# Forget-gate logits of a two-layer trunk: from a TensorE weight chunk to VectorE multiply-and-sum operations

## What is computed

```
def odd_mixer(h, w_in, b_forget, w_out):
    proj = h @ w_in
    fq, fk, fv, fl = jnp.split(proj, [FOX_WIDTH, 2 * FOX_WIDTH, 3 * FOX_WIDTH], axis=-1)
    log_f = jax.nn.log_sigmoid(fl.astype(jnp.float32) + b_forget.astype(jnp.float32))
    o = forgetting_attention(split_heads(fq, FOX_HEADS), split_heads(fk, FOX_HEADS),
                             split_heads(fv, FOX_HEADS), log_f.transpose(0, 2, 1))
    return merge_heads(o).astype(h.dtype) @ w_out
```

## Time and profile before

| | us |
|---|---|
| timed runs, median of 3 (lowest, highest) | 1211.52 (1211.35, 1211.59) |
| profiled execution | 1210.91 |
| its span | 1209.1 |
| TensorE busy | 1197.1 |
| GpSimd busy | 516.9 |
| ScalarE busy | 392.4 |
| VectorE busy | 284.1 |

### The profile page before, as it was taken

The page is one execution under the profiler, slowest core; times in us unless marked ns, Lnnn a source line. Parts: engine busy times, 40 slices in busy tenths (PEclk is TensorE's granted clock), DMA queues, the critical chain, the costliest instruction groups (busy, mean ns, idle before and its releaser), DMA issues.

```text
span 1209.1 us, 14500 instructions
## 1 busy us (share of the span) xinstructions
PE 1197.1 (99%) x5578; PEld 989.9 (82%) x5578; DVE 284.1 (23%) x491; ACT 392.4 (32%) x616; POOL 516.9 (43%) x289
## 2 busy tenths in 40 slices
PE   8999999999999999999999999999999999999998
PEld 6888887898888888888888888678988888888886
DVE  3441056241111111000142325725211101110002
ACT  5122346453223332212242314634433223331210
POOL 5546521744444434444435443033643444435330
PEclk9999999999999999999999999999999999999999
DMA  7444203242223232322224422022322323222211
GB/s 268 132 124 146 95 7 100 70 145 100 100 91 104 87 104 88 103 94 98 70 88 141 173 96 79 18 70 87 105 102 90 104 87 104 88 103 94 98 53 70
DMA packets 34359, 120.14 MB, mean 99 GB/s; under 512 B 3683, under 2 KB 3939, under 8 KB 34316
## 3 DMA queue, kind: packets, MB, share of 16 engines
q1 hardware_dynamic: 30472, 110.46, 26.7%
q10 hardware_dynamic: 3844, 9.07, 2.8%
HBM read 116.09 MB, written 3.42 MB: 99 GB/s over the span
## 4 chain that ended last, share of the span: by engine, by line
PE 98%; DMA 1%; DVE 0%; ACT 0%; POOL 0%; SPq 0%; issue 0%; DVEq 0%; POOLq 0%
PE ps L979 30%; PE ps L981 30%; PE ps L980 30%; PE ps L1175 2%; PE ps L1141 2%; PE ps L1159 1%; PE ps L1006 1%; DMA w_raw<-weights 1%; PE ps L1276 0%; PE ps L1254 0%; PE ps L1139 0%; PE ps L1279 0%; PE ps L1266 0%; POOL w_lo L269 0%; PE ps L1338 0%; PE ps L1337 0%
## 5 line engine op out<-in xcount | busy, mean ns | idle before, releaser
L269 POOL TENSOR_TENSOR w_lo<-w_raw,w_hi 128x1024 fp32r<-128x1024 f32 x199 | 476.5, 2410 | 563.6 <-ACT w_hi L387 562.0
L979 PE MATMUL ps<-h_hi,w_hi 128*128 128x512 f32 (+1 forms) x1008 | 383.0, 380 | 0.0
L981 PE MATMUL ps<-h_hi,w_lo 128*128 128x512 f32 (+1 forms) x1008 | 382.0, 379 | 0.0
L980 PE MATMUL ps<-h_lo,w_hi 128*128 128x512 f32 (+1 forms) x1008 | 382.0, 379 | 0.0
L387 ACT ACTIVATE w_hi<-w_raw 128x1024 fp32r<-128x1024 f32 x201 | 210.1, 1056 | 325.3 <-DMA w_raw<-weights 318.2
L979 PEld LDWEIGHTS ps<-h_hi,w_hi 128*128 128x128 f32 x1008 | 189.6, 188 | 35.7 <-issue 0.3
L981 PEld LDWEIGHTS ps<-h_hi,w_lo 128*128 128x128 f32 x1008 | 189.6, 188 | 35.5
L980 PEld LDWEIGHTS ps<-h_lo,w_hi 128*128 128x128 f32 x1008 | 189.6, 188 | 35.4
L979 PE MATMUL ps<-w_hi,prod_hi 128*128 128x512 f32 x352 | 137.1, 390 | 0.0
L981 PE MATMUL ps<-w_hi,prod_lo 128*128 128x512 f32 x352 | 136.9, 389 | 0.0
L980 PE MATMUL ps<-w_lo,prod_hi 128*128 128x512 f32 x352 | 136.9, 389 | 0.0
(11 more groups left out here) (123 smaller groups left out, 715.2 us busy)
## 6 DMA issues: line engine op xcount, KB each, us to landing
w_raw<-weights SPq DMA_DIRECT2D x201, 512.0 KB, 3.2
x<-x_in SPq DMA_DIRECT2D x4, 512.0 KB, 6.6
gain_post<-norms ACTq DMA_DIRECT2D x4, 512.0 KB, 4.2
minus_f<-forget_rows ACTq DMA_DIRECT2D x1, 2048.0 KB, 11.5
gain_pre<-norms ACTq DMA_DIRECT2D x3, 512.0 KB, 4.1
out<-x SPq DMA_DIRECT2D x3, 512.0 KB, 2.6
bias_rows<-bias_row ACTq DMA_DIRECT2D x1, 1280.0 KB
rel<-bias_rows ACTq DMA_DIRECT2D x1, 1024.0 KB, 5.5
```

Source lines behind the costliest of these rows:

```text
L269: nc.gpsimd.tensor_tensor(w_lo[:, c % RING], w_raw[:, c % RING], w_hi[:, c % RING].bitcast(F32), ALU.subtract).then_inc(lo_done, 1)
L979: mm(to, held[0], moved[0], start=start, stop=False)
L980: mm(to, held[0], moved[1], start=False, stop=False)
L981: return mm(to, held[1], moved[0], start=False, stop=stop)
```

## The change

The gate chunk leaves the stream (200 chunks are left). The 8 gate columns come as rows (`gate_rows`, 8x1024), each broadcast to all 128 partitions: heads 0 to 3 into `gate_w_a`, heads 4 to 6 into `gate_w_b`, head 7 into `gate_w_last`, 4 MB in all, by ScalarE's queue. `boundary(2)` writes its normalized rows to `gate_x`, a buffer of four tiles, instead of `work`. VectorE forms the logits by `tensor_tensor_reduce` over 128x1024: for each group of four heads 16 operations (4 tiles by 4 heads), whose sums fill columns of `gate_z`. TensorE turns four 128x4 blocks of a group into a 4x512 row block (`turn_logits`), group 0 ahead of query/key chunk 1, group 1 ahead of chunk 10. The rest of the gate's work (bias, Exp, Ln, sum, store, spread, mask) is done once for each group on 4 rows or heads.

```diff
-            pe.wait_ge(lo_done, GATE1 + 1)
-
-            for k in range(KT):
-                mm(ps[:, 0, :], w_hi[:, GATE1 % RING, cols(k)], h_hi[:, k, :], start=k == 0, stop=False)
-                last = mm(ps[:, 0, :], w_hi[:, GATE1 % RING, cols(k)], h_lo[:, k, :], start=False, stop=k == KT - 1)
-            last.then_inc(chunk_used, 1)
+
+            def turn_logits(g):
+                pe.wait_ge(gate_dots, 16 * (g + 1))
+                pe.wait_ge(evacuated, qk_first)
+                for t in range(TILES):
+                    n = 16 * g + 4 * t
+                    last = nc.tensor.transpose(ps[0:4, 1 + 2 * g, cols(t)], gate_z[:, n:n + 4], ident[:])
+                last.then_inc(gate_turned, 1)
...
-                    if i == 3:
-                        pe.wait_ge(forget_logit, 1)
+                    if i in (1, 10):
+                        turn_logits(i // 10)
...
+            def dots(g, d0, d1):
+                for d in range(d0, d1):
+                    t, h = d // 4, d % 4
+                    n = 16 * g + d
+                    vec.wait_ge(gate_w_landed[g + (h == 3) if g else 0], 16)
+                    vec.wait_ge(normed, 4 * 2 + t + 1)
+                    if n:
+                        vec.wait_ge(gate_dots, n)
+                    else:
+                        vec.wait_ge(pre_summed, 4 * 2 + 4)
+                    held = gate_w_last[:] if g and h == 3 else gate_w[g][:, h, :]
+                    nc.vector.tensor_tensor_reduce(squares[:], gate_x[:, t, :], held, 1.0, 0.0, ALU.mult, ALU.add,
+                                                   gate_z[:, n:n + 1]).then_inc(gate_dots, 1)
...
+            dots(0, 0, 6)
+            copy_v(0)
+            dots(0, 6, 16)
+            copy_v(1)
+            copy_qk(0)
+            gate_logit(0)
+            dots(1, 0, 2)
+            copy_qk(1)
+            gate_scan(0)
+            dots(1, 2, 4)
+            for i in range(2, 8):
                 copy_qk(i)
...
+                dots(1, 2 * i, 2 * i + 2)
+            copy_qk(8)
+            copy_qk(9)
+            gate_logit(1)
+            add_masks(0)
+            copy_qk(10)
+            gate_scan(1)
+            for i in range(11, LATE):
+                copy_qk(i)
...
-                      {6: lambda: copy_qk(LATE), 9: lambda: copy_qk(LATE + 1)})
+                      {6: lambda: copy_qk(LATE), 9: lambda: copy_qk(LATE + 1), 11: lambda: add_masks(1),
+                       15: lambda: vec.wait_ge(f_masked, 8)})
...
+            act.wait_ge(chunk_used, AFTER[2] - 4)
+            act.dma_start(gate_w[0][:], gate_rows[0:4].partition_broadcast(P)).then_inc(gate_w_landed[0], 16)
+            act.dma_start(gate_w[1][:], gate_rows[4:7].partition_broadcast(P)).then_inc(gate_w_landed[1], 16)
             boundary(2)
...
+            act.dma_start(gate_w_last[:], gate_rows[7].partition_broadcast(P)).then_inc(gate_w_landed[2], 16)
...
+            highs(V1 + AHEAD, QK1 + 8)
+            gate_log(0)
+            high(QK1 + 8)
+            spread_rows(0)
+            highs(QK1 + 9, QK1 + 18)
+            gate_log(1)
+            high(QK1 + 18)
+            spread_rows(1)
+            highs(QK1 + 19, OUT1 + 5)
```

More of the change, by code:

```diff
@@ L73 @@
 V1 = FOUT0 + FT
-GATE1 = V1 + 8
-QK1 = GATE1 + 1
+QK1 = V1 + 8
 OUT1 = QK1 + 2 * FOX
@@ L186, in build @@
             sem(n) for n in ("forget_logit", "forget_log", "f_ready", "f_stored", "f_landed"))
+        gate_w_landed = [sem(f"gate_w_landed{n}") for n in range(3)]
+        gate_dots, gate_turned = sem("gate_dots"), sem("gate_turned")
         ret_k_turned, ret_k_scaled, ret_kv, ret_first, ret_second, ret_state = (
@@ L699, in pre @@
                 q = 4 * b + t
-                row = work[:, 2 * (t % 2):2 * (t % 2) + 2, :].rearrange("p a s -> p (a s)")
+                row = gate_x[:, t] if b == 2 else work[:, 2 * (t % 2):2 * (t % 2) + 2, :].rearrange("p a s -> p (a s)")
                 vec.wait_ge(gain_pre_landed, 16 * (b + 1))
@@ L704, in pre @@
                     vec.wait_ge(x_updated, q - 3)
-                if t >= 2:
+                if t >= 2 and b != 2:
                     vec.wait_ge(h_turned, q - 1)
@@ L915, in _, with gate_logit, gate_scan, copy_v @@
             boundary(2)
-            for half in range(2):
+            def dots(g, d0, d1):
[11 more added lines that the diff above has]
+                                                   gate_z[:, n:n + 1]).then_inc(gate_dots, 1)
+            z, low, neg, one, minus_total = (gate_work[0:4, n, :] for n in range(5))
+            def gate_logit(g):
+                vec.wait_ge(gate_turned, g + 1)
+                own(nc.vector.tensor_scalar(z, ps[0:4, 1 + 2 * g, :], forget_b[0:4, g:g + 1], None, ALU.add))
+                own(nc.vector.tensor_scalar(low, z, 0.0, None, ALU.min))
+                nc.vector.scalar_tensor_tensor(out=neg, in0=low, scalar=2.0, in1=z, op0=ALU.mult,
+                                               op1=ALU.subtract).then_inc(forget_logit, 1)
+            def gate_scan(g):
+                vec.wait_ge(forget_log, g + 1)
+                own(nc.vector.tensor_tensor(z, neg, low, ALU.subtract))
+                own(nc.vector.memset(one, 1.0))
+                if g:
+                    vec.wait_ge(f_stored, 16)
+                nc.vector.tensor_tensor_scan(minus_total, one, z, 0.0, ALU.mult, ALU.add).then_inc(f_ready, 1)
+            def copy_v(half):
                 vec.wait_ge(chunk_used, V1 + 4 * half + 4)
@@ L920, in _ @@
                     evacuate(fox_v[:, t, half * SEQ:(half + 1) * SEQ], 2 * t + half)
[L922 to L933, removed]
             def copy_qk(i):
@@ L936, in copy_qk, with add_masks @@
                 evacuate(fox_qk[:, i, :], qk_bank(i), SCALE if i < FOX else None)
-            for i in range(LATE - 4):
-                copy_qk(i)
[L939 to L944, removed]
+            mask = masks[:, P:2 * P].unsqueeze(1).to_broadcast([P, 4, P])
+            def add_masks(g):
+                vec.wait_ge(f_landed, 16 * (g + 1))
+                heads = slice(4 * g, 4 * g + 4)
+                for j, to in enumerate((masked_f[:, heads], minus_f[:, heads, 5, :], minus_f[:, heads, 0, :],
+                                        minus_f[:, heads, 4, :])):
+                    nc.vector.tensor_tensor(to, minus_f[:, heads, 1 + j, :], mask, ALU.add).then_inc(f_masked, 1)
+            dots(0, 0, 6)
[9 more added lines that the diff above has]
+            for i in range(2, 8):
+                copy_qk(i)
+                dots(1, 2 * i, 2 * i + 2)
[7 more added lines that the diff above has]
+                copy_qk(i)
             vec.wait_ge(f_masked, 4)
@@ L1000, in row_chunk, with rows_of @@
                 return last
+            def rows_of(b, t, k):
+                return gate_x[:, t, cols(k)] if b == 2 else work[:, 2 * (t % 2) + k // 4, cols(k % 4)]
             def turn(b, t):
@@ L1441 @@
     q_and_k = np.concatenate([even[:, :2 * rw], even[:, 4 * rw:4 * rw + 2 * mw]], axis=1)
-    gate = np.concatenate([odd[:, 3 * fw:], np.zeros((DIM, P - FOX), np.float32)], axis=1)
     stream = np.concatenate([
@@ L1446 @@
         *ffn_chunks(ffn_in[0], ffn_out[0]),
-        row_chunks(odd[:, 2 * fw:3 * fw]), column_chunks(gate), column_chunks(odd[:, :2 * fw]),
+        row_chunks(odd[:, 2 * fw:3 * fw]), column_chunks(odd[:, :2 * fw]),
         row_chunks(a(odd_w_out)[0]),
@@ L1461 @@
         "rel_bias": np.concatenate([a(rel_bias), np.ones((1, MOBA), np.float32)]),
-        "forget_bias": a(odd_b_forget)[0][:, None],
+        "forget_bias": a(odd_b_forget)[0].reshape(2, 4).T,
         "ident_in": ident,
```

43 lines of the change are left out of this document (20 added, 23 removed).

## The result

| | us |
|---|---|
| changed kernel, median of 5 (lowest, highest) | 1224.28 (1223.85, 1224.91) |
| kernel before beside it, median of 5 | 1211.52 (1211.17, 1212.58) |
| ratio, 95% interval | 1.0107 (1.0096 to 1.0118) |
| profiled execution, its span | 1223.85, 1222.0 |
| VectorE busy, GpSimd busy | 354.2, 529.4 |

The change costs 12.8 us. The prediction said 1226, in a range of 1209.5 to 1233.

What follows compares the result with a forecast made beforehand. TensorE was taken to bound the kernel, busy in 99% of the span. 1210.91 - 3.65 (matmuls) + 0.97 (transposes) + 13.2 (stall) + 2.5 (clock) + 1.5 (burst) = 1225.4, forecast 1226 us; own range 1220 to 1233, wider range 1209.5 to 1233.

Steps and rivals of the forecast that it cites:

- What bounds the kernel, and the removed matmuls: TensorE is busy in 99% of the span; the sixteen gate matmuls removed are all on the path: -3.65 us.
- A dot alone: One VectorE multiply-and-sum for the gate logits: 1.15 us streaming, 0.14 accumulator read, 0.04 semaphore, 1.33 us in all.
- The dots meet the lows, and alternate: VectorE's multiply-and-sums and GpSimd's low-part subtractions take turns: one dot per 3.52 us while lows are queued.
- Rival (a): Dots do not meet GpSimd's low-part subtractions, so group 0 is hidden: 1210.3 us, no change; chance 0.12.
- (b): Dots do not meet the lows, and the attention's masking burst is hidden too: 1208.8 us, 0.22% faster; chance 0.05.
- (d): A dot streams at half speed, 2.3 us, giving a stall of 31.6 us: 1244 us; chance 0.04.
- (c): VectorE's next dot beats the waiting low, value chunks' lows slip, TensorE stalls 4.6 us: 1216 us; chance 0.09.
- the semaphore gap: Each dot waits for the previous one's semaphore, leaving some 0.18 us in which a queued low takes over.
- The pitch and the stall: Dots every 3.52 us among lows; TensorE waits at group 0's logits turn for dots and value copies: +13.2 us.
- The clock: After the stall at the logits turn, TensorE restarts at a lower clock: +2.5 us (0 to 3).
- The burst in the attention: Group 1's four masking additions, behind VectorE's unit 11, take 2.4 us and delay unit 12: +1.5 us (0 to 2.4).
- Group 1 and the transfers: Second sixteen dots beside query/key copies, and 4 MB of broadcast gate rows on ScalarE's queue: cost 0 each.

Runs made afterwards that it cites:

- experiment 6: Changed kernel with logits turned later (ahead of chunks 4 and 12 instead of 1 and 10), second value copies behind the ninth dot: 1211.13 us, ratio 0.9999.

## Why the prediction was right, point by point

- **What bounds the kernel, and the removed matmuls.** Held. 14 of the 16 gave 3.1 us by themselves.
- **A dot alone.** Priced at 1.33 us, it is 1.41 from one start to the next (672.61 and 674.02 in the profile after): the read of the sum costs 0.08 instead of 0.14, the semaphore 0.17 instead of 0.04.
- **The dots meet the lows, and alternate.** Held, and it decides: without reading lows, or with one input, the stall is gone. Rival (a), that this class of operation reads otherwise, fell, and so did (b) on the same ground; the half-rate dot (d) fell by the 1.23 us; (c), that the next dot beats the waiting low, fell by the row of lows at 3.16 us each, none of them pushed out.
- **The reason given for it failed.** I put the alternation down to the semaphore gap. It holds without that gap and without anything between the operations. Rival (c) was set aside for this reason alone, so that part of the forecast came out for a wrong reason, and that is luck. "Remove the gap and it is 4.6 us" would have been wrong advice.
- **The pitch and the stall were mis-sized, 11.55 us instead of 13.2.** I added the whole stream of a dot (1.15 us) to the low; the measured pitch of 3.34 leaves 3.34 - 2.37 = 0.97 for it. For eleven dots that met a low this takes 11 x 0.18 = 2.0 us off the end; the late start puts 0.9 back, and five dots at 1.41 instead of 1.33 another 0.4: 676.0 - 2.0 + 0.9 + 0.4 = 675.3, measured 675.2. That the twelfth low (665.44) came 0.3 us behind the start of dot 10 (665.12) only changed which dot meets it, 11 instead of 10; eleven dots met a low, as forecast. TensorE was free for the turn at 666.25, 0.9 later than forecast, which is the late start, and began it at 677.80, 0.7 earlier.
- **The clock.** Forecast +2.5 from the start of the run; it was 1.2 here and 2.1 in another kernel behind the same stall, inside the 0 to 3 given.
- **The burst in the attention.** Forecast +1.5, was +1.9: the wait of 1.43 as computed, and 0.5 more in the steps around it. Splitting it into slack took the wait away.
- **Group 1 and the transfers, both at zero.** Held: no other wait of TensorE appeared. The first two pieces of the 4 MB, issued at 595.5 and 595.9, landed in 7.3 and 10.7 us, over 20 us ahead of the first dot.
- **What the sum left out.** A later start, 0.9 us in the profile after and 0.3 to 1.1 at the same place in the other kernels with the DRAM input more.
- **How near the total came.** It lies 1.7 us under the forecast, because the terms erred both ways: -1.65 for the stall and -1.3 for the clock, +0.4 for the burst and +0.9 for the start. The mechanism held; that the total is this near is in part luck. The range of 1220 to 1233 that the prediction gives for the forecast alone does not follow from its own bounds: a stall of 9 and no restart give 1226 - 4.2 - 2.5 = 1219.3, a stall of 17 and a restart of 3 give 1226 + 3.8 + 0.5 = 1230.3. The result lies inside either.

## What to carry to other kernels

Before putting an elementwise operation with two SBUF inputs on VectorE, see what GpSimd does in that stretch: in these runs, while GpSimd had reading work queued, each such operation cost one of GpSimd's instructions on top of its own time, and each of GpSimd's one of VectorE's. The remedy that cost next to nothing was not to make the operations faster but to ask for their results later: with the turn three chunks on, the masks in real slack and the new input at the end, the same idea is 0.2% faster than the kernel before instead of 1.1% slower.

## What the runs showed of the hardware that was not expected

The two engines take strict turns, one instruction each, without any gap to let the other in: pitch 3.34 us for a low of 2.37 and an operation of 1.15 to 1.23, so that 0.2 us of the two overlap.

The meeting was already in the kernel before, hidden. Its cumulative sum, with two SBUF inputs, ran beside a low; in the changed kernel it runs alone:

```profile
671.05 3.10 DVE L933 TENSOR_TENSOR_SCAN gate_work<-gate_work 8x512 f32<-8x512 f32 x1
...
670.68 2.39 POOL L269 TENSOR_TENSOR w_lo<-w_raw,w_hi 128x1024 fp32r<-128x1024 f32 x1 [9.08 <-ACT w_hi L387]
```

```profile
688.01 1.21 DVE L955 TENSOR_TENSOR_SCAN gate_work<-gate_work 4x512 f32<-4x512 f32 x1
```

3.10 us against 1.21 for the same 512 steps: 670.68 + 2.39 = 673.07 is the low's end, and the sum ends 1.1 us behind it. The first has 8 rows and the second 4, a difference in partitions, so that this is read, not tried. The addition ahead of the sum shows that 4 rows are held up as well: alone it takes 0.68 us on 8x512 (at 669.69 in the profile before), and 2.56 on 4x512 where it starts inside a low (experiment 6, at 688.99 in a low from 688.61 to 691.01). Such a record, far longer than its kin and ending one own duration behind a GpSimd instruction, was the mark to look for in the trace of before.
